# Another order for the copies of finished half tiles and for the first gate and up products in a hybrid decoder layer

## The chip, the cores and the metric

The kernel runs on one core of one Trainium2 chip. The metric is the device time of one execution in microseconds. Below, TensorE is PE (its weight loads PEld), VectorE is DVE, ScalarE is ACT, GpSimd is POOL, and SP issues the DMAs. A time difference of about 0.2% is what a measurement of this kernel can tell from none.

## What is computed

One decoder layer on 1024 tokens of width 1024, in float32. The mixing part has three groups of heads; the rest is a gated feed-forward part:

```python
h = rms_norm(x, ln_attn_pre[l])
mix = hybrid_mixer(h, w_in[l], ...)   # NSA | sliding window | stick-breaking heads
x = x + rms_norm(mix @ w_out[l], ln_attn_post[l])
h = rms_norm(x, ln_ffn_pre[l])
f = (jax.nn.silu(h @ ffn_w_gate[l]) * (h @ ffn_w_up[l])) @ ffn_w_down[l]
x = x + rms_norm(f, ln_ffn_post[l])
```

Stick-breaking heads need a log, a scan along the keys and an exponential per row; the window and selection heads need a softmax.

## The kernel before

Every float32 product is made of three products of rounded parts: high by high, high by low, low by high. So each operand is cut: ACT writes the high part, DVE subtracts it from the source and writes the low part. TensorE then runs six or twelve matmuls of 512 columns on them.

**Projection.** `h @ w_in` is computed transposed, in 13 column tiles of 128 output features and two halves of 512 tokens each: 26 halves. A half is four pieces of six matmuls (`piece`, L916), all into one PSUM bank, and from the eleventh half on every half uses the same bank 6. Each half that is finished is copied out of PSUM by ACT (`half_keep`, L1133), scaled by POOL (`half_scale`, L818), and, for keys, cut again. So the first piece of the next half waits until that copy is made (`pe.wait_ge(half_kept, ...)`). The weights of a tile are loaded in two items, whose high parts ACT cuts (`cut_hi`, L1117) and whose low parts DVE makes (`cut_lo`, L1304); three items are held, so a `cut_hi` waits until the pieces of the item three before are done. An item ends at the end of a half or two pieces before it, so in every second case the same piece releases a `half_keep` and a `cut_hi`.

**Attention.** The later halves are interleaved with the attention jobs: `scores` (L997 to L1005), for stick-breaking `stick_exp` (ACT, L1214), `stick_log` (ACT, L1221), `stick_soft` (DVE, L1415), `stick_scan` (DVE, L1423), `stick_sub` (DVE, L1430), `stick_weights` (ACT, L1226); for the others `logits` (DVE, L1407) and `softmax` (ACT, L1202). Then `turn` (PE transposes, L1032), `keep` (a copy to SBUF by ACT, L1232, or DVE, L1437), `weigh` (PE, L1052) and `combine` (DVE, L1467 or L1473). Near the end come the cuts of `w_out`: `out_hi` (ACT, L1266), `out_lo` (DVE, L1497), the first four of which are released by the last piece.

The order of all this on each engine is not written out but planned when the program is built. `plan_attention` lists every item with its engine, an assumed cost, what it needs, and a number called its age. It then always takes the item that can begin first, and among those that can begin at the same time the one with the lowest age:

```python
begin = max(at, free_at[e] if e != "dma" else at)
key = (begin, work[k][3], k)
```

The cuts of the projection's weights and the copies of its halves all have age -100, attention items have ages that grow with the job. With equal ages the name decides, and `cut_hi` comes ahead of `half_keep`. Some of the `keep` items may go to ACT or DVE, whichever is free first by the plan. Each engine then runs its list in that order and waits by semaphores; the numbers of the plan play no part any more.

**Feed-forward.** Gate and up products are done with a seven-product scheme on 2x2 blocks (`P1` to `P7` for each of 22 units, `product`, L2409), down products in the same manner (L2439). The products P1 and P2 of the first four units come first, since they need only tokens that are ready early. The last token tile's transposes (`turn(NT - 1)`, L2343) stand between the fourth product and the fifth. Here the order on ACT and DVE is written by hand, ahead of the loop over all products:

- ACT: `cut_hi` (L1956, high part of weights for one product), `top_cut` (L1933, high part of sums of token blocks), `hidden_raw` (L1905, copies the turned last token tile out of PSUM), `block_hi` (L1914), `snap_first` (L1964, copies P1 of a unit out of PSUM), `silu_first` (L1977), and in the loop `snap_second` (L1969, copies the P6 bank out).
- DVE: `cut_lo` (L2194), `top_rest` (L2188, low parts of the sums), `sums` (L2129 to L2137, the sums themselves), `hidden_cut` (L2119), `first_block` (L2201, adds P2 to P1). The second product P2 in a bank waits for the `first_block` two units before it.

The sixth product needs `first_block(0)`, the eighth `first_block(1)`, the ninth (P6 of unit 0) six of the ten `top_rest`, the tenth (P7) eight, the eleventh (P5) `snap_second(0)`.

## Time and profile before

| | us |
|---|---|
| runs (three) | 1263.75, 1264.02, 1265.2 |
| median | 1264.02 |
| the profiled execution | 1261.04 |
| its span, first to last instruction | 1259.2 |
| mean granted TensorE clock in it | 0.997 |
| busy in it: PE, DVE, ACT, POOL | 1231.5, 866.3, 602.8, 179.1 |

The span is what the rows count; 1.84 us of the profiled execution lie outside it, and that execution was 2.98 us shorter than the median. Times in rows are from the start of the span. In a row of a timeline the first number is the start, the second the duration; the bracket at the end gives the engine's idle time before it and who ended it. "x" is a count.

By the timeline, the first part of the projection runs from 9 us to about 106 us, attention with the interleaved halves from 121 to 520 us, the output product from 520 to 606 us, the gate and up products from 606 to about 1030 us, the down products to 1250 us.

### The profile page before, as it was taken

To read this page: it belongs to the slowest core of one execution; us is meant where nothing else is said; L and a number is where in the kernel's file an instruction comes from. 1 tells how busy PE (TensorE), PEld (TensorE's weight loads), DVE (VectorE), ACT (ScalarE), POOL (GpSimd) and SP (SyncE) were. 2 spreads that over 40 slices of the span, in tenths; PEclk is the share of its full clock that TensorE was granted. 3 is DMA by queue.
4 is the path that set the end of the run, shared out by engine and by line. 5 is a ranking of instruction groups with operands and counts; after the bars stand their busy time and mean duration, and the time that the engine had idled before them with its cause. 6 is when DMAs were issued, how large, how long until landed. Compare 5 with 4: busy or idle time off the path is not lost.

```text
span 1259.2 us, 19142 instructions
## 1 busy us (share of the span) xinstructions
PE 1231.5 (98%) x6744; PEld 1055.9 (84%) x6744; DVE 866.3 (69%) x1656; ACT 602.8 (48%) x1144; POOL 179.1 (14%) x153
## 2 busy tenths in 40 slices
PE   8999999999999999999999999999999999999998
PEld 7899878889988999888778888888888887888886
DVE  6323688859779666355976766656756668796995
ACT  5432677657666565344643333333333436443341
POOL 5230111111100000011001112111212120000104
PEclk9999999999999999999999999999999999999999
DMA  6303512136743000223213333233232367373343
GB/s 233 119 1 119 117 35 51 34 109 169 171 115 88 18 18 18 79 89 115 103 42 109 97 112 100 75 119 125 93 117 85 129 213 275 102 241 93 109 159 134
DMA packets 67171, 136.44 MB, mean 108 GB/s; under 512 B 8663, under 2 KB 27359, under 8 KB 67076
## 3 DMA queue, kind: packets, MB, share of 16 engines
q1 hardware_dynamic: 67076, 135.22, 34.3%
q8 instruction: 54, 0.88, 0.3%
q14 instruction: 41, 0.34, 0.1%
HBM read 89.81 MB, written 28.60 MB: 94 GB/s over the span
## 4 chain that ended last, share of the span: by engine, by line
PE 84%; DVE 8%; issue 3%; ACT 3%; DMA 1%; SPq 0%; POOL 0%; DVEq 0%; POOLq 0%; ACTq 0%
PE ps L2409 32%; PE ps L2439 15%; PE ps L1052 7%; PE ps L2353 6%; PE ps L1032 4%; PE ps L897 4%; PE ps L916 4%; PE ps L842 3%; PE ps L997 2%; PE ps L1005 2%; DVE ring L1423 2%; PE ps L931 1%; PE ps L1063 1%; DVE ring L1415 1%; DVE m_rows_sb L1430 1%
## 5 line engine op out<-in xcount | busy, mean ns | idle before, releaser
L2409 PE MATMUL ps<-f_topH,f_W 128*128 128x512 f32 x704 | 220.8, 389 | 0.8 <-ACT QT L1969 0.8
L2409 PEld LDWEIGHTS ps<-f_topH,f_W 128*128 128x128 f32 x704 | 132.1, 188 | 28.6 <-DVE f_W L2194 1.1
L2409 PE MATMUL ps<-f_topL,f_W 128*128 128x512 f32 x352 | 136.9, 389 | 0.0
L1052 PE MATMUL ps<-V,m_tw 128*128 128x66 f32 (+1 forms) x1056 | 129.6, 271 | 2.7 <-DVE m_mix_n L1467 1.7
L1052 PEld LDWEIGHTS ps<-V,m_tw 128*128 128x128 f32 x1056 | 126.5, 192 | 4.5 <-DVE m_mix_n L1467 2.5
L2439 PE MATMUL ps<-f_headH,f_W 128*128 128x512 f32 x408 | 128.0, 390 | 0.0
L2409 PE MATMUL ps<-f_headH,f_W 128*128 128x512 f32 x352 | 115.0, 390 | 2.4 <-DVE f_p1a L2201 2.4
L2194 DVE TENSOR_TENSOR f_W<-f_scr,f_W 128x512 fp32r<-128x512 f32 x88 | 62.1, 708 | 78.6 <-ACT f_W L1956 78.4
L2194 DVE TENSOR_TENSOR f_W<-ring,f_W 128x512 fp32r<-128x512 f32 (+1 forms) x84 | 76.0, 914 | 46.2 <-ACT f_W L1956 46.2
L2439 PEld LDWEIGHTS ps<-f_headH,f_W 128*128 128x128 f32 x408 | 76.6, 188 | 15.9 <-DVE f_headL L2237 0.2
L2409 PEld LDWEIGHTS ps<-f_headH,f_W 128*128 128x128 f32 x352 | 66.1, 188 | 16.4 <-issue 2.8
L2439 PE MATMUL ps<-f_headL,f_W 128*128 128x512 f32 x204 | 79.4, 389 | 0.0
L2409 PEld LDWEIGHTS ps<-f_topL,f_W 128*128 128x128 f32 x352 | 66.1, 188 | 13.6
L1232 ACT COPY m_tw<-ps 128x512 f32<-128x512 f32 (+1 forms) x97 | 53.5, 567 | 49.6 <-PE ps L1052 28.2
L2409 PE MATMUL ps<-f_headL,f_W 128*128 128x512 f32 x176 | 68.5, 389 | 0.0
L2439 PE MATMUL ps<-f_b22H,f_W 128*128 128x512 f32 x208 | 66.6, 392 | 0.9 <-DVE QT L2229 0.9
L916 PE MATMUL ps<-m_hH,m_wH 128*128 128x512 f32 x144 | 60.3, 419 | 4.9 <-ACT QT L1133 4.8
L2229 DVE TENSOR_TENSOR QT<-ps,QT 128x512 f32<-128x512 f32 x67 | 46.0, 687 | 27.4 <-PE ps L2439 27.3
L2353 PE MATMUL ps<-o_w,o_mH 128*128 128x512 f32 x224 | 60.5, 392 | 0.0
L2409 PE MATMUL ps<-f_b22H,f_W 128*128 128x512 f32 x176 | 57.8, 389 | 0.0
L916 PE MATMUL ps<-m_hH,m_wL 128*128 128x512 f32 x144 | 57.2, 397 | 0.0
L916 PE MATMUL ps<-m_hL,m_wH 128*128 128x512 f32 x144 | 56.9, 395 | 0.0
(288 smaller groups left out, 2727.9 us busy)
## 6 DMA issues: line engine op xcount, KB each, us to landing
act_pairs<-QT SPq DMA_DIRECT2D x77, 256.0 KB, 3.9
f_stage<-act_pairs SPq DMA_DIRECT2D x77, 256.0 KB, 2.6
m_qs<-m_qn SPq DMA_DIRECT2D x128, 128.0 KB, 2.4
ring<-in_ffn_w_up SPq DMA_DIRECT2D x22, 512.0 KB, 3.7
ring<-in_ffn_w_gate SPq DMA_DIRECT2D x19, 512.0 KB, 5.0
ring<-in_w_in_tiles SPq DMA_DIRECT2D x9, 512.0 KB, 3.6
ring<-in_nsa_phi_w SPq DMA_DIRECT2D x8, 512.0 KB, 4.7
ring<-in_w_out SPq DMA_DIRECT2D x8, 512.0 KB, 5.0
```

Of the source, the lines that this page charges most:

```text
L842: return pe.matmul(ps[:, h, :], w[:, k % W_ITEMS, (h // 2) * P:(h // 2 + 1) * P], a[:, k, half_cols(h)], start=first, stop=last)
L897: ins = pe.matmul(ps[:, b + a, 0:VW_HALF], h[:, k, tok], wv[:, w, k, a * VW_HALF:(a + 1) * VW_HALF], start=(k == 0 and h is hH and w == 0) ...
L916: ins = pe.matmul(ps[:, bank, :], w[:, n % W_ITEMS, cols], a[:, k, hf * HALF:(hf + 1) * HALF], start=(k == 0 and w is wH and a is hH), sto ...
L997: pe.matmul(out, q_hi_, k, start=True, stop=False)
L1032: ins = pe.transpose(ps[:, bank, i * P:(i + 1) * P], rows, ident[:])
L1052: ins = pe.matmul(ps[:, SUMS, wide * i:wide * (i + 1)], tw[:, t % W_SLOTS, P * i:P * i + P], v, start=(kb == 0 and i == 0), stop=(kb == jo ...
L1232: act.copy(out, src).then_inc(kept_by["act"], 1)
L2194: dve.tensor_tensor(slots[s % W_RING][:, 1, 0:n], source(s), slots[s % W_RING][:, 0, 0:n].bitcast(F32), ALU.subtract).then_inc(lo_done, 1)
L2229: dve.tensor_tensor(part, product_, part, ALU.add).then_inc(y_added, 1)
L2353: ins = pe.matmul(ps[:, 2 * (t % 2) + hf, :], m[:, t % 2, k, :], w[k][:, a, hf * HALF:(hf + 1) * HALF], start=(k == 0 and m is mH and a == ...
L2409: ins = pe.matmul(ps[:, bank, :], whole[:, w, cols], halves[h][:, k0 + k, col:col + HALF], start=(begins and k == 0 and w == 0 and h == 0) ...
L2439: ins = pe.matmul(ps[:, bank, :], whole[:, w, k * P:(k + 1) * P], block(n)[h], start=(begins and k == 0 and w == 0 and h == 0), stop=(k == ...
```

## The change

Two things, no instruction is added or taken away.

1. In the planner, `half_keep` on ACT gets the age -200 in place of -100. A finished half is now copied ahead of a `cut_hi` that could begin at the same time. Since the planner takes one item after the other, all that comes behind moves too: the lists of all five engines are different from about 130 us to 500 us. Two more of the 164 `keep` items go to ACT and two fewer to DVE.
2. In the hand-written order at the start of the feed-forward part, ACT cuts the weights of the sixth and seventh product ahead of the last token tile, and DVE adds the first block ahead of some sums and low parts.

```diff
@@ plan_attention @@
-            add(("half_keep", h), "act", act(HALF), [("piece", s), ...], -100)
+            add(("half_keep", h), "act", act(HALF), [("piece", s), ...], -200)
             add(("half_scale", h), "pool", 1650, [("half_keep", h)], -100)
@@ act_program @@
         top_cut(2)
         cut_hi(4)
+        cut_hi(5)
+        top_cut(3)
+        cut_hi(6)
+        snap_first(1)
         hidden_raw(NT - 1)
         block_hi(NT - 1)
-        cut_hi(5)
-        top_cut(3)
-        snap_first(1)
         top_cut(4)
-        cut_hi(6)
+        cut_hi(7)
         top_cut(5)
-        cut_hi(7)
-        silu_first(0)
         cut_hi(8)
         top_cut(6)
+        silu_first(0)
+        cut_hi(9)
         top_cut(7)
         snap_first(2)
-        cut_hi(9)
@@ dve_program @@
         normalise(t)
+        cut_lo(4)
+        first_block(0)
         sums(2, (1,))
-        cut_lo(4)
+        cut_lo(5)
         top_rest(1)
-        top_rest(2)
+        cut_lo(6)
         sums(3, (0,))
-        cut_lo(5)
         hidden_cut(t)
         sums(3, (1,))
-        first_block(0)
-        cut_lo(6)
+        top_rest(2)
+        first_block(1)
+        cut_lo(7)
         top_rest(3)
+        sums(2, (2,))
         top_rest(4)
-        cut_lo(7)
         top_rest(5)
-        first_block(1)
-        sums(2, (2,))
         cut_lo(8)
         sums(3, (2,))
         top_rest(6)
+        cut_lo(9)
         top_rest(7)
-        cut_lo(9)
```

How it moves the instructions at three places:

**The end of a half in the stick-breaking stage.** On TensorE, at the end of the sixteenth half (half 15) and the start of half 16; - is before, + is the change. L916 are the pieces, L1052 is `weigh`, L997 to L1005 are `scores`:

```order
 L1002 MATMUL ps<-m_mask_sb,m_identr 128x128
 L1005 MATMUL ps<-m_KSb,m_qs 128x512
-L1052 MATMUL ps<-V,m_tw 128x64 x4
+L1052 MATMUL ps<-V,m_tw 128x64 x8
+L916 MATMUL ps<-m_hH,m_wH 128x512
+L916 MATMUL ps<-m_hL,m_wH 128x512
+L916 MATMUL ps<-m_hH,m_wL 128x512
+L916 MATMUL ps<-m_hH,m_wH 128x512
+L916 MATMUL ps<-m_hL,m_wH 128x512
+L916 MATMUL ps<-m_hH,m_wL 128x512
 L916 MATMUL ps<-m_hH,m_wH 128x512
 L916 MATMUL ps<-m_hL,m_wH 128x512
```

The last piece of half 15 stood earlier, among the transposes of an attention job; now it is directly ahead of the first piece of half 16. On ACT the copy of half 15 (L1133) and the weights' high part beside it (L1117), before:

```order
L1221 ACTIVATE ring<-ring 128x768
L1232 COPY m_tw<-ps 128x512
L1117 CAST m_wH<-ring 128x512
L1133 ACTIVATE QT<-ps 128x512
L1232 COPY m_tw<-ps 128x512 x3
L1232 COPY QT<-ps 128x2x128
L1226 ACTIVATE m_rows_sb<-m_rows_sb 128x768 x2
```

and now:

```order
L1242 COPY m_mix_a<-ps 128x256
L1214 ACTIVATE ring<-ps 128x256
L1252 ACTIVATE m_junk,m_ss<-m_mix_a 128x256
L1133 ACTIVATE QT<-ps 128x512
L1117 CAST m_wH<-ring 128x512
L1221 ACTIVATE ring<-ring 128x768
```

The copy now stands ahead of the cut, and both stand behind the squares of a mixed tile (L1252) instead of ahead of three `keep` copies.

**The cuts of w_out.** On ACT, where the smallest jobs of the last family begin; L1266 is `out_hi`, before:

```order
L1252 ACTIVATE m_junk,m_ss<-m_mix_a 128x512
L1202 ACTIVATE m_rows_cmp<-m_rows_cmp,m_neg 128x15 x4
L1266 CAST o_w<-ring 128x1024
L1196 CAST m_qn<-QT 128x2x128
L1266 CAST o_w<-ring 128x1024
L1232 COPY m_tw<-ps 128x512
L1232 COPY m_tw<-ps 128x256
L1266 CAST o_w<-ring 128x1024
L1202 ACTIVATE m_rows_win<-m_rows_win,m_neg 128x256 x4
L1266 CAST o_w<-ring 128x1024
L1202 ACTIVATE m_rows_slc<-m_rows_slc,m_neg 128x256 x4
```

and now:

```order
L1202 ACTIVATE m_rows_slc<-m_rows_slc,m_neg 128x128 x3
L1266 CAST o_w<-ring 128x1024
L1202 ACTIVATE m_rows_slc<-m_rows_slc,m_neg 128x128
L1266 CAST o_w<-ring 128x1024 x2
L1196 CAST m_qn<-QT 128x2x128
L1266 CAST o_w<-ring 128x1024
L1232 COPY m_tw<-ps 128x256
L1252 ACTIVATE m_junk,m_ss<-m_mix_a 128x512
L1202 ACTIVATE m_rows_cmp<-m_rows_cmp,m_neg 128x15 x4
```

The four `out_hi` stood between the `keep` copies and the softmax rows of 128x256; now they stand ahead of the rows of 128x15. The four `out_lo` on DVE moved ahead in the same way.

**The first feed-forward products.** On DVE, behind the normalising of the last token tile; L2194 is `cut_lo`, L2188 `top_rest`, L2201 `first_block`, L2129 to L2137 `sums`:

```order
 L2129 TENSOR_TENSOR QT<-QT 128x4x128
 L2108 SCALAR_TENSOR_TENSOR o_tmp<-ring,o_rs,o_gpre 128x1024
+L2194 TENSOR_TENSOR f_W<-f_gates,f_W 128x512
+L2201 TENSOR_TENSOR f_p1a<-ps,f_p1a 128x512
 L2133 TENSOR_TENSOR QT<-QT 128x4x128
 L2194 TENSOR_TENSOR f_W<-f_gates,f_W 128x512
-L2188 TENSOR_TENSOR f_topL<-QT,f_topH 128x8x128 x2
+L2188 TENSOR_TENSOR f_topL<-QT,f_topH 128x8x128
+L2194 TENSOR_TENSOR f_W<-f_gates,f_W 128x512
 L2129 TENSOR_TENSOR QT<-QT 128x4x128
-L2194 TENSOR_TENSOR f_W<-f_gates,f_W 128x512
 L2119 TENSOR_TENSOR f_b22L<-QT,f_b22H 128x4x128
```

`first_block(0)` moved ahead of three sums, two low parts of 128x8x128, a `cut_lo` and a `hidden_cut`, and the low parts follow later, one by one.

## Rows read from the trace of the kernel before

**Rows 1.** The page: busy time, share of the span, instructions.
```profile
PE 1231.5 (98%) x6744; PEld 1055.9 (84%) x6744; DVE 866.3 (69%) x1656; ACT 602.8 (48%) x1144; POOL 179.1 (14%) x153
```

**Rows 2.** View of waits, TensorE: who for whom, total us, times, longest.
```profile
PE ps L916 <- ACT QT L1133: 4.8, 4, 2.3
PE ps L2409 <- DVE f_p1a L2201: 2.4, 1, 2.4
...
PE ps L1052 <- DVE m_mix_n L1467: 1.7, 2, 1.1
...
PE ps L1052 <- ACT m_tw L1232: 0.9, 1, 0.9
...
PE ps L1032 <- ACT m_rows_win L1202: 0.7, 1, 0.7
```

**Rows 3.** Stretches: busy us of each engine (x instructions), PEclk, DMA share, GB/s.
```profile
121.00:270.00 149.00, 141.14 (x828) 120.41 (x828) 119.86 (x157) 101.01 (x208) 24.82 (x20) 0.99 0.25 63
270.00:360.00 90.00, 89.76 (x693) 84.55 (x692) 69.09 (x263) 58.20 (x152) 8.45 (x12) 1.00 0.63 153
360.00:370.00 10.00, 9.65 (x71) 8.69 (x71) 6.70 (x31) 5.71 (x17) 0.54 (x1) 1.00 0.25 58
370.00:395.00 25.00, 20.88 (x155) 18.67 (x154) 24.35 (x99) 19.52 (x46) 1.08 (x2) 1.00 0.54 158
...
606.00:640.00 34.00, 30.89 (x140) 25.06 (x139) 31.89 (x47) 24.47 (x39) 1.84 (x2) 1.00 0.22 78
```

**Rows 4.** Timeline of TensorE: first products behind an idle time, 170 to 262 us.
```profile
175.49 0.48 PE L916 MATMUL ps<-m_hH,m_wH 128*128 128x512 f32 x1 [1.35 <-ACT QT L1133]
...
190.96 0.47 PE L916 MATMUL ps<-m_hH,m_wH 128*128 128x512 f32 x1 [1.00 <-ACT QT L1133]
...
232.55 0.47 PE L916 MATMUL ps<-m_hH,m_wH 128*128 128x512 f32 x1 [2.28 <-ACT QT L1133]
...
260.06 0.30 PE L997 MATMUL ps<-m_KSa,m_qs 128*128 128x128 f32 x1 [1.19 <-DVE m_rows_sb L1430]
```

**Rows 5.** Timeline of ACT just ahead of the third of them.
```profile
231.31 0.60 ACT L1117 CAST m_wH<-ring 128x512 fp32r<-128x512 f32 x1
231.81 0.59 ACT L1133 ACTIVATE QT<-ps 128x512 f32<-128x512 f32 x1
```

**Rows 6.** Stretch behind the third, columns as in rows 3.
```profile
233.00:237.00 4.00, 4.00 (x13) 3.08 (x12) 3.97 (x5) 0.95 (x1) 1.07 (x1) 0.57 0.00 0
```

**Rows 7.** Timeline of POOL and of DVE at two half ends.
```profile
232.48 1.59 POOL L818 TENSOR_TENSOR QT<-QT 128x512 f32<-128x512 f32 x1 [2.96 <-ACT QT L1133]
...
232.92 1.70 DVE L1304 TENSOR_TENSOR m_wL<-ring,m_wH 128x512 fp32r<-128x512 f32 x1
...
175.44 0.68 DVE L1304 TENSOR_TENSOR m_wL<-ring,m_wH 128x512 fp32r<-128x512 f32 x1
```

**Rows 8.** Timeline of ACT, 370 to 372 us.
```profile
370.23 1.04 ACT L1266 CAST o_w<-ring 128x1024 fp32r<-128x1024 f32 x1
371.18 0.85 ACT L1232 COPY m_tw<-ps 128x512 f32<-128x512 f32 x2
```

**Rows 9.** Timeline of DVE, 391 to 394 us.
```profile
391.63 1.22 DVE L1497 TENSOR_TENSOR o_w<-ring,o_w 128x1024 fp32r<-128x1024 f32 x1
393.17 0.42 DVE L1467 TENSOR_TENSOR m_mix_n<-ps,m_coef 128x256 f32<-128x256 f32 x1
```

**Rows 10.** Timeline of TensorE in the first feed-forward products: idle times.
```profile
622.95 0.47 PE L2409 MATMUL ps<-f_headH,f_W 128*128 128x512 f32 x1 [2.36 <-DVE f_p1a L2201]
...
637.55 0.47 PE L2409 MATMUL ps<-f_topH,f_W 128*128 128x512 f32 x1 [0.75 <-ACT QT L1969]
```

**Rows 11.** Timeline of DVE and ACT around them.
```profile
622.12 0.69 DVE L2201 TENSOR_TENSOR f_p1a<-ps,f_p1a 128x512 f32<-128x512 f32 x1
...
634.55 0.68 DVE L2201 TENSOR_TENSOR f_p1b<-ps,f_p1b 128x512 f32<-128x512 f32 x1
...
636.83 0.57 ACT L1969 COPY QT<-ps 128x512 f32<-128x512 f32 x1
```

More of the change, by code:

```diff
@@ L244, in plan_attention @@
         elif s % 4 == 3:
-            add(("half_keep", h), "act", act(HALF), [("piece", s), ("half_lo", h - 10 if kind == "k" else 21) if h >= 20 else None], -100)
+            add(("half_keep", h), "act", act(HALF), [("piece", s), ("half_lo", h - 10 if kind == "k" else 21) if h >= 20 else None], -200)
             add(("half_scale", h), "pool", 1650, [("half_keep", h)], -100)
```

## The prediction

> **What bounds it now.** I read the page's totals first, then the waits of TensorE, the busy times by stretch, and the timeline at each wait. TensorE is busy 98% of the span [rows 1], and the change adds and removes no instruction, so the time can change only by TensorE's idle time, by its clock, and by little else. The stretches say where idle time is left: 7.9 us between 121 and 270 us (149.00 less 141.14), 0.2 in the next 90 us, 0.4 from 360 to 370, 4.1 from 370 to 395, and 3.1 from 606 to 640 [rows 3]. These are the places that the two edits touch. Elsewhere a new order moves work that TensorE hides.
>
> **Ends of halves, 121 to 270 us.** TensorE waited 4.8 us in four places for the copy of a half [rows 2]: 1.35 us at the opening of half 14, 1.00 at half 15, 2.28 at half 18 [rows 4], which leaves 0.2 for the fourth, at half 12. At the third ACT made the weights' cut at 231.31 and began the copy at 231.81 [rows 5]: the cut ahead of it costs 0.5 us. Behind that wait the clock was 0.57 of full over 4.00 us [rows 6], that is, it stood at 1.2 in place of 2.4 GHz for most of it, which costs 4.00 x 0.43 = 1.7 us of work. Now, half by half, from the order of the changed kernel:
> - Half 12: the cut is behind the copy, the wait of 0.2 goes: -0.2.
> - Half 14: the cut is behind, -0.5, and one `scores` pair of about 0.5 us now stands in the gap: -1.0 of 1.35.
> - Half 15: no cut stood ahead of the copy, 0.
> - Half 18: the copy loses the cut, -0.5, so 1.8 us stay. The clock did not fall behind 1.35 us here (0.99 over the stretch is the one fall) [rows 3, 4], nor behind 2.36 us at 622.95, where it is 1.00 [rows 3, 10], but did behind 2.28. I take it as gone: -1.7. Its other end is 0.
> - Halves 16 and 22: work stood between the last piece of the half before and the first of these; now there is none. Each costs a bare opening, 1.00 us as at half 15 [rows 4]: +2.0.
> - Half 20 is now directly behind half 19 too, but there TensorE stood 1.19 us for the scores anyway [rows 4]: -0.2. Half 21 opens behind only 0.6 us of scores: +0.4. Together +0.2.
>
> Sum -0.2 - 1.0 - 0.5 - 1.7 + 2.0 + 0.2 = **-1.2 us**. From 270 to 360 us TensorE has no idle time [rows 3], so what is won before arrives at 360 unabridged.
>
> **The cuts of w_out, 360 to 395 us.** DVE is full there, 24.35 of 25.00 us, and had 3.3 us free in the ten before [rows 3]. By the new order the last piece stands ahead of the last eight `scores` before it and releases the four `out_hi` (1.04 us each, [rows 8]) and `out_lo` (1.22, [rows 9]) earlier. Behind them stood: the copy of a transposed block at 371.18, directly behind an `out_hi` [rows 8], waited for 0.9 us; softmax rows, 0.7; and two combines, one at 393.17 behind an `out_lo` at 391.63 [rows 9], together 1.7 [rows 2]. So 3.3 us of TensorE's idle time stand directly behind a cut. Against it: the pieces that filled TensorE up to there end sooner, and two `out_lo`, 2.4 us, now stand ahead of the last combine of the sliding-window jobs, for which TensorE must wait; half of that, 1.2 us, I take as new idle time. -3.3 + 1.2 = -2.1, rounded to **-2.0 us**. The ends: all of 4.1 + 0.4 gone, -4.5; or all of the 2.4 new and only one of the cuts' waits gone, +1.5.
>
> **POOL beside DVE.** Each copy releases POOL's scaling. At 232.48 POOL began 0.44 us ahead of DVE's low part, and that took 1.70 us; at 175.44 DVE began together with it and took 0.68 [rows 7]. With the copy ahead of the cut, POOL begins first each time: 1.0 us more on DVE at five half ends or so (9, 11, 13, 19, 21), 5 us at most. TensorE waits for DVE rarely there (1.19 us at half 19 is the one large wait in rows 4), so I put **+0.5 us** on the path; the ends are 0 and +5. The Trainium skill, page "SBUF — State Buffer", section "Who interferes with whom", says that a VectorE instruction with two SBUF inputs and a GpSimd one that reads SBUF lock each other out, and the one issued first holds the shared ports to its end; by that rule every one of the five is paid in full, and the rows agree for the two places shown. It speaks against this change, and is a rival below.
>
> **First feed-forward products, 606 to 640 us.** TensorE waited 2.36 us ahead of the sixth product for `first_block(0)`, made at 622.12, and 0.75 ahead of the eleventh for `snap_second(0)` [rows 10, 11]. The edit puts the first block ahead of seven other DVE items, and cuts the sixth product's weights inside an idle time of ACT, so the wait of 2.36 goes. But what is late next? The eleventh product waits for ACT's copy at 636.83; ahead of that on ACT stands a silu that needs `first_block(2)`, which DVE began at 634.55 [rows 11]. Between the normalising of the last tile and 634.55 DVE has the same instructions before and after, only in another order, and it is the full engine: 31.89 of 34.00 us [rows 3]. So `first_block(2)` comes at about the same time, and so do the copy and the eleventh product. The idle time moves: Stepping the new DVE list from the normalising on, with 0.6 to 0.7 us for a 128x512 item [rows 11] and 1.2 for a 128x1024 one [rows 9], the eighth low part is there after 16.8 us, and TensorE at the tenth product, with five products of 12 matmuls behind the last tile's turn, after 15.5: I expect 1.3 us idle ahead of the tenth and the other 1.8 ahead of the eleventh. Only a DVE idle moment can be won: **-0.2 us**. The ends are -0.7 (the wait of 0.75 goes) and +1.7 (a clock fall as in rows 6, for two near waits in place of one).
>
> **Sum.** -1.2 - 2.0 + 0.5 - 0.2 = -2.9 us. The profiled execution took 1261.04, so its like would take 1258.1; the median of the runs lies 2.98 above it: 1264.02 - 2.9 = **1261.1 us**. About 0.2%, 2.5 us, is what a measurement can tell from none; the bound is 1261.5, so this is barely a gain.
>
> **Rivals.**
> 1. *The full DVE only passes its idle time on.* The cuts of w_out delay the last sliding-window combines as much as they free the later ones; the term of -2.0 is 0: 1263.1. For it: DVE is full at 370 to 395 and its total does not change [rows 3]. Against: 3.3 free us just ahead. Chance 0.23.
> 2. *POOL's lock on the path.* All five low parts pay 1.0 and stick-breaking rows wait behind them: the term is +5 in place of +0.5, 1265.6. For it: rows 7. Against: TensorE waits little for these rows [rows 4]. Its rule is that of the page named above. Chance 0.10.
> 3. *Slower: bare openings as at half 18.* If ACT is busy with stick-breaking rows when halves 16 and 22 end, each wait is 2.28 and not 1.00, and if the clock falls behind both as in rows 6, each costs 1.7 more: 2 x (1.28 + 1.7) = +6.0, so 1267.1. It decides from a wait of about 2.3 us on, since 1.35 left the clock alone. For it: ACT is busy 101 of 149 us there [rows 3]. Against: half 15 opened bare with 1.00. Chance 0.13.
> 4. *The change doesn't do what it says.* The plan's costs are assumed; if ACT is in fact free whenever a half ends, copy and cut differ by 0.5 us that nobody waits for, and the rest is chance: 1264.0. Against: at half 18 the cut did stand ahead [rows 5]. Chance 0.06.
>
> **Numbers.** The forecast has 0.48; its own range by the terms is 1257 to 1261.5. Faster by more than 0.2%: 0.48. Within: 0.23 + 0.10 + 0.06 = 0.39. Slower: 0.13. The range leaves out the end of rival 3 and the case in which all of 4.5, 2.9 and 0.7 goes: 1256.5 to 1266.0.
>
> **What would show it.** In the new profile: the wait for the copy of a half at half 14 is at most 0.4 us and at half 18 below 1.8, with full clock behind it; new waits of about 1 us stand at halves 16 and 22. Idle time from 121 to 270 us is some 8 us. From 360 to 395 TensorE idles some 2.5 us in place of 4.5, with no `out_hi` behind 368 us. There is no wait ahead of the sixth product, two ahead of the tenth and eleventh with about 3 us together, and the eleventh begins as long after the last tile's normalising as before, within 0.3 us. The low parts beside POOL take 1.7 us. The prediction is wrong if the sum of TensorE's idle time falls by less than 2 us, or more than 6, or if the change is found where I see none, behind 395 us.

## The result, and the profile after

The changed kernel is slower: 1266.37 us at the median of 20 runs, against 1263.74 for 20 runs of the kernel before on the same chips. The ratio is 1.0024 with a 95% interval of [1.0016, 1.0032]. The prediction was 1261.1.

The executions list a mean granted clock each, so time can be split for all of them. I call **clock loss** the span times one minus that clock, and **rest** the time less the clock loss. Half of any idle time that passes while the clock is down counts as loss. The figures are means over the executions of a kernel, without one of about 2070 us of the change and one of x6:

| | executions | mean time | clock loss | rest |
|---|---|---|---|---|
| before (the runs beside the experiments) | 128 | 1263.3 | 6.2 | 1257.1 |
| after | 19 | 1266.6 | 8.5 | 1258.1 |

Of 3.3 us, 2.3 are clock and 1.0 is the rest. The standard error is 0.4 and 0.2 us for the change. The 128 executions were taken on four chips, whose means are 1262.3, 1263.1, 1263.5 and 1263.9 us (rest 1257.0, 1256.7, 1257.2, 1257.3). So a difference of under 1 us between means of different chips shows little, and each ratio below is to before on the same chip.

The profiled execution of the changed kernel took 1269.17 us (span 1267.4, clock 0.991), longer than its median. Its busy times, as in [rows 1]:

```profile
PE 1237.9 (98%) x6744; PEld 1061.6 (84%) x6744; DVE 863.5 (68%) x1654; ACT 604.5 (48%) x1146; POOL 181.3 (14%) x153
```

Its stretches, as in [rows 3]:

```profile
121.00:270.00 149.00, 140.41 (x824) 119.05 (x823) 116.53 (x155) 102.13 (x210) 26.04 (x20) 1.00 0.26 64
270.00:360.00 90.00, 88.40 (x675) 82.32 (x673) 67.99 (x250) 56.48 (x147) 8.51 (x12) 1.00 0.61 152
360.00:370.00 10.00, 8.63 (x72) 8.07 (x71) 8.21 (x32) 7.57 (x16) 0.00 (x0) 1.00 0.49 141
370.00:395.00 25.00, 20.30 (x134) 19.03 (x134) 19.76 (x85) 14.54 (x37) 2.00 (x2) 0.80 0.44 134
...
606.00:640.00 34.00, 34.00 (x159) 28.06 (x157) 31.95 (x44) 22.66 (x35) 2.41 (x4) 1.00 0.27 97
```

From 121 to 270 us the clock is full now, and idle time is 8.6 us, where it was 7.9. From 360 to 395 it is 6.1, where it was 4.5, and the clock has fallen to 0.80. From 606 to 640 there is none, because this part now runs some 8 us later: its waits lie at 641 and 645 us (below). The waits of TensorE, as in [rows 2]:

```profile
PE ps L916 <- ACT QT L1133: 5.5, 8, 1.0
PE ps L1021 <- DVE m_mix_a L1487: 3.5, 1, 3.5
PE ps L997 <- DVE m_rows_sb L1430: 3.1, 4, 1.5
PE ps L1052 <- ACT m_tw L1232: 2.2, 2, 2.1
PE ps L2409 <- ACT QT L1969: 1.6, 1, 1.6
...
PE ps L2409 <- issue: 1.0, 1, 1.0
```

The second line is new. The third was 1.9 us before, the fourth 0.9 [rows 2]. The one wait of 3.5 us is for the norm of the last sliding-window tile (`norm_mix`, L1487), whose transposes (L1021) TensorE runs next. The timeline of TensorE around it:

```profile
370.69 0.69 PE L1052 MATMUL ps<-VC,m_tw 128*128 128x132 f32 x4 [2.06 <-ACT m_tw L1232]
...
376.21 1.09 PE L1021 MATMUL ps<-ident,m_mix_a 128*128 128x128 f32 x4 [3.48 <-DVE m_mix_a L1487]
```

and the stretches there, two microseconds each:

```profile
370.00:372.00 2.00, 1.31 (x10) 1.34 (x11) 1.33 (x11) 1.96 (x8) 0.00 (x0) 0.92 0.96 324
372.00:374.00 2.00, 0.73 (x4) 0.44 (x3) 1.93 (x6) 0.00 (x0) 0.26 (x1) 0.50 0.76 303
374.00:376.00 2.00, 0.00 (x0) 0.00 (x0) 1.48 (x2) 0.00 (x0) 1.20 (x1) 0.50 0.69 242
...
380.00:382.00 2.00, 2.00 (x11) 2.00 (x11) 1.78 (x11) 1.34 (x4) 0.00 (x0) 0.52 0.00 0
```

The clock goes to 0.50, 1.2 in place of 2.4 GHz, at 371.7 us (0.92 from 370 to 372 us). That is 1 us behind the end of the first wait, of 2.06 us, and 1 us ahead of the second, of 3.48. It stays down through the second wait and for nearly 6 us of work behind it: the matmuls from 376.2 to 381.9 us take twice their time, which is 2.9 us. So in this execution the norm's wait did not bring the clock down by itself; it stood in a time in which the clock was down already.

The first wait comes from the high parts on ACT. The copy that TensorE waits for stands directly behind the last of four `out_hi`:

```profile
369.24 1.04 ACT L1266 CAST o_w<-ring 128x1024 fp32r<-128x1024 f32 x1
370.18 0.36 ACT L1232 COPY m_tw<-ps 128x256 f32<-128x256 f32 x1
```

Why is the norm late? The chain is combine (L1467), squares (ACT, L1252), mean (L1479), root (POOL, L822), norm (L1487). DVE before:

```profile
364.76 0.42 DVE L1467 TENSOR_TENSOR m_mix_a<-ps,m_coef 128x256 f32<-128x256 f32 x1
...
367.30 0.75 DVE L1487 SCALAR_TENSOR_TENSOR m_mix_a<-m_mix_a,m_rs,m_g_w 128x512 f32<-128x512 f32 x1 [0.73 <-POOL m_rs L822]
```

DVE after:

```profile
366.87 2.47 DVE L1497 TENSOR_TENSOR o_w<-ring,o_w 128x1024 fp32r<-128x1024 f32 x2 [0.15 <-ACT o_w L1266]
...
369.66 0.42 DVE L1467 TENSOR_TENSOR m_mix_a<-ps,m_coef 128x256 f32<-128x256 f32 x1
...
371.64 1.22 DVE L1497 TENSOR_TENSOR o_w<-ring,o_w 128x1024 fp32r<-128x1024 f32 x1
...
373.52 0.14 DVE L1479 TENSOR_SCALAR m_ms<-m_ss 128x1 f32<-128x1 f32 x1
373.58 1.22 DVE L1497 TENSOR_TENSOR o_w<-ring,o_w 128x1024 fp32r<-128x1024 f32 x1
375.31 0.75 DVE L1487 SCALAR_TENSOR_TENSOR m_mix_a<-m_mix_a,m_rs,m_g_w 128x512 f32<-128x512 f32 x1 [0.52 <-POOL m_rs L822]
```

From the end of the combine to the end of the norm it took 2.87 us before, 5.98 after, and the combine itself came 4.90 us later. Two low parts stand ahead of the combine, one ahead of the mean, one behind it. The last one hits the root. POOL before and after:

```profile
366.65 0.54 POOL L822 TENSOR_TENSOR m_rs<-m_ms,m_mhalf 128x1 f32<-128x1 f32 x1 [10.44 <-DVE m_ms L1479]
```

```profile
373.74 1.46 POOL L822 TENSOR_TENSOR m_rs<-m_ms,m_mhalf 128x1 f32<-128x1 f32 x1 [14.89 <-DVE m_ms L1479]
```

The root works on one number per partition. It took 0.92 us more beside a low part that had begun 0.16 us ahead of it, and ended 0.40 us behind that part's end. This is the rule of the Trainium skill, "SBUF — State Buffer", "Who interferes with whom", in the direction that I had not looked at: DVE was first and POOL waited.

And nothing covered it. Before, the last piece of the projection (103) stood in the list of TensorE directly ahead of these transposes, and piece 102 six items ahead of it. The norm ended at 368.05 and the transposes began at 368.72, as soon as the piece was through: no wait, and 0.7 us of slack. Now the last piece ends at 365.34, and from there TensorE has only what hangs on DVE and ACT.

The openings of halves, as in [rows 4]:

```profile
175.43 0.47 PE L916 MATMUL ps<-m_hH,m_wH 128*128 128x512 f32 x1 [0.68 <-ACT QT L1133]
...
207.43 0.47 PE L916 MATMUL ps<-m_hH,m_wH 128*128 128x512 f32 x1 [1.03 <-ACT QT L1133]
...
215.65 0.50 PE L997 MATMUL ps<-m_KSb,m_qs 128*128 128x512 f32 x1 [1.55 <-DVE m_rows_sb L1430]
...
233.07 0.47 PE L916 MATMUL ps<-m_hH,m_wH 128*128 128x512 f32 x1 [0.78 <-ACT QT L1133]
```

And the feed-forward part, as in [rows 10]:

```profile
641.08 0.47 PE L2409 MATMUL ps<-f_topH,f_W 128*128 128x512 f32 x1 [1.02 <-issue]
...
645.71 0.47 PE L2409 MATMUL ps<-f_topH,f_W 128*128 128x512 f32 x1 [1.62 <-ACT QT L1969]
```

### The profile page after: what moved, and what is told of

Its sections match the earlier page's. It is cut to its first block, busy times and chain, and to the rows that moved or that the text cites. A ratio compares the mean times of both kernels' runs of the same rounds, so it can differ in the third digit from the quotient of the medians.

```text
span 1267.4 us, 19142 instructions
## 1 busy us (share of the span) xinstructions
PE 1237.9 (98%) x6744; PEld 1061.6 (84%) x6744; DVE 863.5 (68%) x1654; ACT 604.5 (48%) x1146; POOL 181.3 (14%) x153
## 4 chain that ended last, share of the span: by engine, by line
PE 82%; DVE 9%; issue 3%; ACT 2%; DMA 2%; POOL 1%; SPq 1%; DVEq 0%; POOLq 0%; ACTq 0%
PE ps L2409 31%; PE ps L2439 15%; PE ps L1052 8%; PE ps L2353 4%; PE ps L916 4%; PE ps L1032 4%; PE ps L897 4%; PE ps L842 3%; PE ps L997 3%; PE ps L1005 2%; PE ps L931 1%; DMA m_qs<-m_qn 1%; DVE ring L1423 1%; PE ps L1063 1%; DVE ring L1415 1%
## 5 line engine op out<-in xcount | busy, mean ns | idle before, releaser
L1052 PE MATMUL ps<-V,m_tw 128*128 128x66 f32 (+1 forms) x1056 | 131.9, 274 | 0.4 <-ACT m_tw L1232 0.2
L1052 PEld LDWEIGHTS ps<-V,m_tw 128*128 128x128 f32 x1056 | 128.9, 194 | 3.0 <-issue 0.7
L2194 DVE TENSOR_TENSOR f_W<-f_scr,f_W 128x512 fp32r<-128x512 f32 x88 | 62.1, 708 | 78.2 <-ACT f_W L1956 78.1
L2194 DVE TENSOR_TENSOR f_W<-ring,f_W 128x512 fp32r<-128x512 f32 (+1 forms) x84 | 76.0, 914 | 46.9 <-ACT f_W L1956 46.9
L916 PE MATMUL ps<-m_hH,m_wH 128*128 128x512 f32 x144 | 60.2, 418 | 5.5 <-ACT QT L1133 5.5
L1956 ACT CAST f_W<-ring 128x512 fp32r<-128x512 f32 (+1 forms) x84 | 50.6, 606 | 13.7 <-PE ps L2439 9.8
L818 POOL TENSOR_TENSOR QT<-QT 128x512 f32<-128x512 f32 x24 | 34.4, 1446 | 156.1 <-ACT QT L1133 147.6
```

Source lines behind the costliest of these rows:

```text
L916: ins = pe.matmul(ps[:, bank, :], w[:, n % W_ITEMS, cols], a[:, k, hf * HALF:(hf + 1) * HALF], start=(k == 0 and w is wH and a is hH), sto ...
L1052: ins = pe.matmul(ps[:, SUMS, wide * i:wide * (i + 1)], tw[:, t % W_SLOTS, P * i:P * i + P], v, start=(kb == 0 and i == 0), stop=(kb == jo ...
L1956: act.copy(slots[s % W_RING][:, 0, 0:n], source(s)).then_inc(hi_done, 1)
L2194: dve.tensor_tensor(slots[s % W_RING][:, 1, 0:n], source(s), slots[s % W_RING][:, 0, 0:n].bitcast(F32), ALU.subtract).then_inc(lo_done, 1)
```

## The experiments

Below, the *tail* is the end of the sliding-window jobs, 360 to 400 us, and a *bare opening* is the first piece of a half directly behind the last piece of the half before, with no other work between. The expectations name theories. **T1**: the early cuts of w_out make the last sliding-window norm late, and the clock falls. **T2**: the bare openings of halves cost the time. **T3**: the last pieces come too early and no longer cover the norm. **F**: the feed-forward edit only moves idle time and wins about 0.4 us. **C**: a late norm costs its wait and, mostly, a clock fall. **I**: idle time only. **O**: the opening of half 16 costs the time. Each kernel ran 12 times, beside the kernel before on the same chip. In x3, x6 and x8 line numbers are one higher than in the change, in x11 two; in x9, x10 and x13 they are two higher from L1487 on.

| | ratio to before [95%] | mean | clock loss | rest | norm wait | waits 360–400 |
|---|---|---|---|---|---|---|
| before | 1 | 1263.3 | 6.2 | 1257.1 | 0 | 4.4 |
| after | 1.0024 [1.0016, 1.0032] | 1266.6 | 8.5 | 1258.1 | 3.48 | 6.0 |
| x1 ffn edit only | 0.9977 [0.9962, 0.9993] | 1260.9 | 4.7 | 1256.2 | 0 | 4.2 |
| x2 plan edit only | 1.0034 [1.0019, 1.0050] | 1267.9 | 10.7 | 1257.3 | 2.59 | 5.2 |
| x3 cuts held | 1.0036 [1.0018, 1.0054] | 1268.5 | 7.4 | 1261.1 | 1.88 | 6.2 |
| x4 halves under 16 | 1.0002 [0.9985, 1.0019] | 1263.8 | 4.2 | 1259.6 | 0 | 4.8 |
| x5 halves from 16 | 1.0021 [1.0009, 1.0034] | 1266.3 | 7.8 | 1258.5 | 3.88 | 6.7 |
| x6 pieces held | 1.0018 [1.0004, 1.0032] | 1265.5 | 5.3 | 1260.2 | 1.35 | 4.4 |
| x7 half 13 only | 0.9996 [0.9985, 1.0007] | 1262.6 | 6.0 | 1256.6 | 0 | 4.2 |
| x8 low parts held | 1.0009 [0.9999, 1.0018] | 1264.3 | 5.8 | 1258.5 | 1.33 | 4.7 |
| x9 norm late, 20 spare | 1.0000 [0.9987, 1.0014] | 1263.2 | 6.5 | 1256.7 | 1.93 | 6.1 |
| x10 norm late, 10 spare | 0.9992 [0.9980, 1.0005] | 1262.3 | 4.9 | 1257.3 | 0.60 | 5.0 |
| x11 both held | 1.0012 [0.9997, 1.0027] | 1264.8 | 4.0 | 1260.8 | 1.34 | 4.7 |
| x12 all but half 15 | 1.0024 [1.0009, 1.0040] | 1265.8 | 8.2 | 1257.6 | 3.54 | 6.1 |
| x13 norm late, 40 spare | 1.0037 [1.0020, 1.0054] | 1267.2 | 7.6 | 1259.6 | 4.49 | 7.8 |
| x14 halves under 15 | 0.9997 [0.9983, 1.0010] | 1261.9 | 3.7 | 1258.2 | 0 | 4.2 |

The last two columns are of the profiled execution: the wait ahead of the transposes L1021 of the last sliding-window tile, and all waits of TensorE over 0.2 us from 360 to 400. Standard errors of x1 to x14: 0.4 to 0.8 us for the clock loss (1.0 in x3), 0.2 to 0.55 for the rest. Means include all executions, and the first row is the mean of four chips, so means can stand some tenths off the ratio.

**x1 and x2: the two edits apart.** x1 has the hand-written lists of the change and the old age (the diff shows it against the change); x2 has the new age and the lists of before.

```diff
-            add(("half_keep", h), "act", act(HALF), [("piece", s), ("half_lo", h - 10 if kind == "k" else 21) if h >= 20 else None], -200)
+            add(("half_keep", h), "act", act(HALF), [("piece", s), ("half_lo", h - 10 if kind == "k" else 21) if h >= 20 else None], -100)
```

> Only the second edit (the order of the first feed-forward products); the planner as before. Theory F (the edit moves TensorE's idle time and wins little): 0.4 us less than the kernel before, ratio 0.9997; the waits are about 1.0 us ahead of the tenth product and 1.6 ahead of the eleventh, in place of 2.4 ahead of the sixth. Rival (two near waits lower the clock): 1 to 2 us more than before.

> Only the first edit (the age of the copies of halves). If the slowdown is the planner's alone: 3 us more than the kernel before, ratio 1.0027, with a wait of 3 to 4 us of TensorE for the norm of the last sliding-window tile (DVE m_mix_a L1487) near 376 us. If the two edits hurt together only: within 1 us of before.

The feed-forward edit is a gain by itself, 0.9977 [0.9962, 0.9993]; the plan edit a loss, 1.0034 [1.0019, 1.0050]. The sign lies in the plan. Multiplied, the two ratios give 1.0011, with an error of about 0.0022, where the change has 1.0024: they add up within the noise and no better. x1 is below the 0.9997 of theory F by more than its interval. In x2 the wait for the norm is 2.59 us, under the 3 to 4 expected. The waits of x1 are those of the change in this part, and its rest is 0.5 us and its clock loss 1.7 us under those of before on the same chip:

```profile
630.46 0.47 PE L2409 MATMUL ps<-f_topH,f_W 128*128 128x512 f32 x1 [1.01 <-issue]
...
635.08 0.47 PE L2409 MATMUL ps<-f_topH,f_W 128*128 128x512 f32 x1 [1.65 <-ACT QT L1969]
```

**x3: cuts of w_out held back.** Behind the copy of the turned last sliding-window tile.

```diff
- add(("out_hi", k), "act", act(D), [("out", k), room], 1e5)
+ held = ("keep", lay.turn_at["swa", NT - 1]) if k < OUT_EARLY else None
+ add(("out_hi", k), "act", act(D), [("out", k), room, held], 1e5)
```

> The changed kernel, but the planner may place the first four high parts of w_out only behind the keep copy of the last sliding-window tile; the lists are those of the changed kernel up to there. Theory T1 (the early cuts of w_out make the last sliding-window norm late, and the idle time lowers the clock): the wait of 3.5 us at 376 us and the one of 2.1 us at 371 are gone, the clock stays at 1.00 there, time 0 to 3 us below the kernel before, ratio 0.998 to 1.000. Theory T2 (the bare openings of halves 16, 20 and 22 cost the time): still 2 to 3 us above before, ratio 1.002.

```profile
370.37 0.63 PE L1022 MATMUL ps<-ident,m_mix_a 128*128 128x128 f32 x4 [1.88 <-DVE m_mix_a L1488]
...
380.83 1.11 PE L1053 MATMUL ps<-V,m_tw 128*128 128x66 f32 x8 [1.36 <-DVE m_mix_n L1468]
...
395.94 0.33 PE L1053 MATMUL ps<-V,m_tw 128*128 128x66 f32 x1 [1.45 <-DVE m_mix_n L1468]
```

No gain: 1.0036 [1.0018, 1.0054]. With no low part in the way the root took 0.54 us, the norm wait fell to 1.88 and the wait of 2.06 us was gone (0.70 for a combine stood there), but the held cuts then stood ahead of later work, and TensorE waited 0.83, 1.36 and 1.45 us for combines. The clock, which T1 wanted at 1.00, fell to 0.50 behind the 1.88 us, from 370.9 to 374.3 us. T1 in its simple form fell. The rest of x3, 3.0 us over that of the change, is not explained by its waits, which are as long.

**x4 and x5: the new age for some halves only.**

The end of the `half_keep` line in x4; in x5 the condition is `h >= 16`:

```diff
-[("piece", s), ("half_lo", h - 10 if kind == "k" else 21) if h >= 20 else None], -200)
+[("piece", s), ("half_lo", h - 10 if kind == "k" else 21) if h >= 20 else None], -200 if h < 16 else -100)
```

> The changed kernel, but the new age only for halves below 16: bare openings at halves 16 and 20, none at 22, and the cuts of w_out stand as in the kernel before. T1: no long wait at 371 to 376 us, time within 1.5 us of before (ratio 0.999 to 1.001). T2: one bare opening fewer of three, so 1.5 to 2 us above before (ratio 1.0012 to 1.0018).

> The changed kernel, with the new age of the copies kept only for halves 16 and later; halves before 16 have the age of before. T3 (new, after the held cuts left 6.2 us of waits in 360 to 400: the last pieces of the last half, which before stood between the turn of the last sliding-window tile and the nsa jobs as filler, are now done before it, and nothing covers the chain combine, squares, mean, root, norm, turn): nearly the whole loss is here, ratio 1.001 to 1.004, a wait of 2.5 to 3.6 us for the norm of the last sliding-window tile near 376, 5.5 to 6.5 us of waits of over 0.2 us in 360 to 400, with a clock fall behind them in most executions. T2 (bare openings at halves 16, 20 and 22): the same order, 1.000 to 1.003, but its waits are near 215, 259 and 283, and those in 360 to 400 explain under 1 us. If the loss needs the halves before 16, the ratio is under 0.999.

x5 has the tail of the change and nearly all of its loss, 1.0021 [1.0009, 1.0034]; its clock loss is 7.8 us, its norm wait 3.88.

x4 has the tail of before and no norm wait, and the lowest clock loss but two, 4.2. Its ratio, 1.0002 [0.9985, 1.0019], is in T1's range and leaves T2's open. Its rest speaks for T2: it is 2.5 us over the one of before, and 3.4 over x1, which ran on the same chip and differs from it by the age of these halves alone. Its timeline shows where:

```profile
206.53 0.47 PE L916 MATMUL ps<-m_hH,m_wH 128*128 128x512 f32 x1 [1.02 <-ACT QT L1133]
...
214.74 0.50 PE L997 MATMUL ps<-m_KSb,m_qs 128*128 128x512 f32 x1 [1.57 <-DVE m_rows_sb L1430]
...
232.75 0.47 PE L916 MATMUL ps<-m_hH,m_wH 128*128 128x512 f32 x1 [1.35 <-ACT QT L1133]
```

The opening of half 16 and the scores behind it wait 2.6 us that were not there before; waits over 0.2 us from 121 to 270 sum to 9.4 us, before 7.2. A further 1.21 us near 302 us is a wait for a DMA of queries, of which more below.

**x6: pieces 102 and 103 held** behind the turns that they followed before.

```diff
+ needs += [("turn", lay.turn_at["swa", NT - 1] - 2 + s - PIECES + 1)] if s >= PIECES - 2 else []
  add(("piece", s), "pe", 6 * 226.5, needs, 1e4 + s)
```

> The changed kernel, with the last two pieces (102 and 103) held in the plan behind the turns that they followed before; the w_out cuts, which need piece 103, then come late too. All other openings are as in the change. T3: the wait for the norm near 376 falls to under 1 us, waits in 360 to 400 sum to 4 to 5 us as before, the ratio is 0.998 to 1.001, that is 2 to 5 us under the change. T2: the early openings cost as they do in the change, ratio 1.001 to 1.004, with the tail repaired for under 1.5 us of it.

The norm wait is 1.35, where T3 wanted under 1, the waits at the tail are those of before in sum (4.4 us), and the clock loss is 3.2 us under the change. But the rest is 2.0 us over it, so that 1.0018 [1.0004, 1.0032] is left, in T2's range and above T3's. Most of the 2.0 may be a matter of counting: in the profiled execution of the change the clock was down for all of the wait of 3.48 us, so 1.7 us of idle time stand there under clock loss, and in x6 none do. T3 has the mechanism of the clock loss, and not the whole time.

**x7: half 13 alone** has the new age.

```diff
-[("piece", s), ("half_lo", h - 10 if kind == "k" else 21) if h >= 20 else None], -200)
+[("piece", s), ("half_lo", h - 10 if kind == "k" else 21) if h >= 20 else None], -200 if h in (13,) else -100)
```

> The changed kernel with the new age for the copy of half 13 alone: pieces in the order of before from half 17 or so on, the w_out cuts as before, the ffn edit in. T3: 0.9965 to 0.999, as the ffn edit alone, tail waits 4 to 5 us. T2: one opening moved to be covered (14), one new bare one (17): within 1 us of the ffn edit alone either way. If the gain of the new age at half 14 that the prediction booked (1.0 us) is real, it is the fastest so far, near 0.997.

0.9996 [0.9985, 1.0007], above all that was expected: the opening of half 14 waits less (0.78 us), but half 17 opens bare for 0.78. The rest is 0.4 us over x1, which is within the noise; of the 1.7 us in the mean 1.3 are clock loss.

**x8: low parts held** behind the norm; **x11: that and the pieces.**

```diff
+ behind = ("norm_mix", 2 * NT - 1) if k < OUT_EARLY else None
- add(("out_lo", k), "dve", dve(D), [("out_hi", k)], 1e5)
+ add(("out_lo", k), "dve", dve(D), [("out_hi", k), behind], 1e5)
```

> The changed kernel with the four low parts of w_out held on VectorE behind the norm of the last sliding-window tile; ScalarE's high parts stay early, and so do the last pieces. T1 in its port form (the root on GpSimd took 1.46 us beside a low part, and VectorE's low parts push the norm back): the root takes about 0.54 us, the wait for the norm falls by 2 to 3 us, ratio 0.999 to 1.002. T3: the root falls to 0.54 us too and the norm wait by about 1.5 us as in the held-cuts kernel, but the idle time goes to later items: 360 to 400 still sums to 5 to 6.5 us and the ratio is 1.001 to 1.004.

```profile
370.67 0.54 POOL L823 TENSOR_TENSOR m_rs<-m_ms,m_mhalf 128x1 f32<-128x1 f32 x1 [12.32 <-DVE m_ms L1480]
```

```profile
372.23 0.63 PE L1022 MATMUL ps<-ident,m_mix_a 128*128 128x128 f32 x4 [1.33 <-DVE m_mix_a L1488]
```

```profile
368.00:370.00 2.00, 0.87 (x8) 0.78 (x7) 1.41 (x10) 2.00 (x4) 0.00 (x0) 1.00 0.92 324
370.00:372.00 2.00, 0.90 (x8) 0.69 (x6) 1.93 (x9) 1.19 (x6) 0.54 (x1) 1.00 0.08 31
```

> The changed kernel with both repairs of the end of the sliding-window jobs: pieces 102 and 103 held behind the turns that they followed before, and the low parts of w_out held behind the norm. The bare openings of halves 15, 16, 20 and 22 stay. Theory C: no norm wait over 1.4 us, clock's loss 5 to 6 us as in the two single repairs (5.3 and 5.8). Time without the clock's loss stays 2 to 3.5 us over the one of before, because of the bare openings; ratio 1.0005 to 1.002. If the openings cost nothing, the ratio is under 0.9995.

x8 undoes the least: the high parts stay early on ACT, the root takes 0.54 us again, the wait is 1.33 in place of 3.48, and the clock stays at 1.00 though TensorE idles 2.2 of 4 us. One thing more moved: the plan gave the copy behind the fourth high part to DVE (L1438), so that the wait of 2.06 us became 1.13. What each of the two shorter waits did for the clock x8 does not tell apart. Clock loss falls by 2.7 us, the mean time by 2.3, the ratio is 1.0009 [0.9999, 1.0018]. The port form of T1 named these numbers; T3, which wanted 5 us of waits from 360 to 400, got 4.7. x11 loses only 4.0 us to the clock (5 to 6 expected), and its rest is 3.7 us over before (2 to 3.5 expected); ratio 1.0012 [0.9997, 1.0027]. So the repairs of the tail give the clock back, and leave time that lies elsewhere; holding the pieces adds to it (x6 and x11 against the change and x8: 2.0 and 2.2 us of rest). The counting above can be 1.7 of the first 2.0; for x11 against x8 it explains nothing, and what those 2.2 us are was not found.

**x9, x10 and x13: a late norm by itself.** The plan of before, the feed-forward edit, and 20, 10 or 40 spare DVE instructions ahead of that one norm.

```diff
+ for q in range(20 if i == 2 * NT - 1 else 0):
+     dve.scalar_tensor_tensor(out=spare[:, 2 * q:2 * q + 2], in0=gain_of(family)[:, 0:2], scalar=rs[:, i:i + 1], in1=gain_of(family)[:, 0:2], op0=ALU.mult, op1=ALU.mult)
```

> The ffn edit alone, with the plan of before, and 20 spare VectorE instructions of 128x2 ahead of the norm of the last sliding-window tile (some 0.15 us each, 3.0 us in all; they write to a buffer that nothing reads). The order of all other work is the one of before. It measures what a late norm at this place costs, by itself. Theory C (a late norm costs its wait and, in most executions, a clock fall): with 0.4 us of slack at the turn, a wait of 2.2 to 2.8 us for the norm near 367, time without the clock's loss up by 2 to 2.8 us on the ffn edit alone, and the clock's loss (span times one minus the mean granted clock) up from 4.7 us to 6.5 or more: ratio 1.0005 to 1.003. Theory I (idle only; where the clock falls has nothing to do with this wait): the clock's loss stays at 4.7 to 5.5 us, ratio 0.9995 to 1.0005. If the wait is made up by later idle time, the ratio stays under 0.999.

> As the kernel with 20 spare instructions, with 10 (1.5 us). A wait of about 1.1 us for the norm. Theory C: time without the clock's loss up by 0.8 to 1.2 us, the clock's loss up by at most 1 us (the waits of 0.9 to 1.4 us at this place in other kernels of this study stood beside a mean loss of 5.3 to 5.8 us). Theory I: the same in idle time, the clock's loss unchanged.

> The ffn edit alone, with the plan of before, and 40 spare VectorE instructions ahead of the norm of the last sliding-window tile (128x1; the 20 of 128x2 gave a wait of 1.93 us at the turn, so some 4.5 us here, or 3 us if the narrower ones are cheaper). Theory C (the late norm brings the clock down): the clock's loss 8 us or more, as in the change (8.5), and a clock fall at 370 to 380 in the profiled run; time in all up by 5 to 7 us on the ffn edit alone, ratio 1.002 to 1.004. Theory I (idle time only): clock's loss 4.5 to 6 us, up by 2.5 to 4.5 us in all, ratio 1.000 to 1.0015.

```profile
370.21 0.63 PE L1021 MATMUL ps<-ident,m_mix_a 128*128 128x128 f32 x4 [1.93 <-DVE m_mix_a L1489]
```

```profile
373.41 0.99 PE L1021 MATMUL ps<-ident,m_mix_a 128*128 128x128 f32 x4 [4.49 <-DVE m_mix_a L1489]
```

```profile
370.00:372.00 2.00, 0.00 (x0) 0.00 (x0) 2.00 (x17) 0.05 (x1) 0.00 (x0) 1.00 0.94 254
...
374.00:376.00 2.00, 1.74 (x8) 1.34 (x7) 2.00 (x4) 1.31 (x3) 0.00 (x0) 0.50 0.04 8
```

Against x1, waits of 0.60, 1.93 and 4.49 us cost 1.4, 2.3 and 6.3 us in the mean, and the clock loss rose by 0.2, 1.8 and 2.9 us. These are means of different chips; by the ratios, each to before on its own chip, the three cost 1.9, 2.9 and 7.6 us. The clock fell behind the wait of 4.49 and not behind 1.93 in the profiled executions. So a norm that is late by itself, with the attention lists as before, makes the kernel as slow as the plan edit did, 1.0037 [1.0020, 1.0054], and nearly half of that is clock. Theory C holds in x13, with a clock loss 0.4 us under the 8 that it wanted. In x9 it had the clock loss (6.5) and not the time: the rest rose by 0.5 us and not by 2, and 1.0000 [0.9987, 1.0014] lies in theory I's range. x10's 1.2 us of rest are twice its wait; its profiled execution also shows two waits for a DMA of queries (1.24 us the longest, near 302 us), as x4 and x6 have and the one of before has not. x9 and x13, whose order is the same up to there, have none, so such waits come and go with the execution, and up to 2 us of a profiled execution's rest can be theirs.

**x12: all but half 15; x14: halves under 15 only.** x12 first:

```diff
-[("piece", s), ("half_lo", h - 10 if kind == "k" else 21) if h >= 20 else None], -200)
+[("piece", s), ("half_lo", h - 10 if kind == "k" else 21) if h >= 20 else None], -100 if h in (15,) else -200)
```

```diff
-[("piece", s), ("half_lo", h - 10 if kind == "k" else 21) if h >= 20 else None], -200)
+[("piece", s), ("half_lo", h - 10 if kind == "k" else 21) if h >= 20 else None], -200 if h < 15 else -100)
```

> The changed kernel with the age of before for the copy of half 15 alone, which opens half 16 later. Theory O (the bare opening of half 16 and the row of scores that then waits, 1.0 and 1.55 us near 207 and 215, are lost time): those two waits shrink by 1.5 to 2.5 us in sum and the time by as much, ratio 1.0005 to 1.002 with the late norm still there (wait of about 3.5 us near 376, clock's loss 8 to 9 us). If they are covered later, as the openings of halves 20 and 22 seem to be, the ratio stays at 1.002 to 1.003.

> The changed kernel with the new age only for halves 14 and earlier. Theory O: with half 15's copy at the age of before, the waits of 1.0 us at half 16's opening (near 207) and 1.55 us at the scores after it (near 215) shrink by 1.5 us or more in sum; the time without the clock's loss falls from 1259.6 (new age for all halves below 16) to 1257.5 to 1258.3, ratio 0.998 to 1.0. If those waits only move to the opening's next place, as they did in the kernel with half 15 alone at its old age (1.53, 0.35 and 0.47 us between 210 and 218), the time without the clock's loss stays above 1258.8 and the ratio at 0.9995 to 1.001.

```profile
205.50 0.47 PE L916 MATMUL ps<-m_hH,m_wH 128*128 128x512 f32 x1 [1.54 <-ACT QT L1133]
...
213.19 0.50 PE L997 MATMUL ps<-m_KSb,m_qs 128*128 128x512 f32 x1 [0.46 <-DVE m_rows_sb L1430]
```

The waits at half 16 did not go, they split: 1.54, 0.34 and 0.46 in place of 1.02 and 1.57. x14's rest is 1258.2, 1.4 under x4 (0.35 standard error), and x12's 0.5 under the change, which is within the noise; the ratio of x12, 1.0024 [1.0009, 1.0040], is that of the change, and that of x14 is 0.9997 [0.9983, 1.0010]. x4 and x14 ran on different chips; measured from before on its own chip, the rest is 2.9 and 1.2 us up, 1.7 apart. So half 15's copy is part of the cost of the early halves in x14, and x12 neither shows nor excludes it in the change; theory O had the rest of x14 right and the waits that should show it wrong. Which opening costs the change its 1 us of rest stays open.

## Why the prediction was wrong

The step that failed is **"the cuts of w_out"**, booked at -2.0 us with +1.5 as its worse end. It named both forces: pieces that end sooner, and two low parts ahead of the last combine. It priced the second as "half of that, 1.2 us" of idle time and stopped at the combine. Behind the combine come squares, mean, root, norm and transposes, on three engines, and low parts stood ahead of the mean and beside the root too. The norm moved from 367.30 to 375.31. Of the 3.3 us that were booked as gone, 2.4 did go: the softmax rows (0.74) and the combines (0.64 and 1.06). The copy behind an `out_hi` did not: the high parts moved ahead of another copy, and its wait rose from 0.92 to 2.06. The norm's 3.48 came on top. So the new idle time was 4.6 us and not 1.2, and in place of -2.0 the waits from 360 to 395 rose by 1.6 us. And this term had no price for the clock behind such waits. In the mean the clock loss is 2.3 us over before; against kernels that, like the change, have no long wait at half 18 but the tail of before (x4 4.2, x14 3.7) it is over 4. In x8, with the low parts held, it is 2.7 us lower.

**Rival 3** had the right sign, near the right time (1267.1) and the right kind of price, a long wait and then a slow clock. Its place was wrong: halves 16 and 22 opened after 1.03 and 0.77 us, as the forecast itself had them. And its rule, that it decides from a wait of about 2.3 us on, does not hold: the clock stayed up behind 2.36 us at 622.95 [rows 10], and it fell behind 1.88 us in x3 and 1.34 and 1.38 us in x6.

**Ends of halves.** Half 14: 1.35 to 0.68, forecast -1.0, was -0.7, so over the 0.4 that the text allowed it. Half 18: 2.28 to 0.78, more than the 0.5 forecast, with the clock at full behind it. Halves 16, 22 and 21: 1.03, 0.77, 0.37 (forecast 1.0, 1.0, 0.4). Half 20: 1.19 to 0.78. Half 15: 1.00 to 0.78, forecast no change. So the openings came out as read or better, except half 14's and a new wait of 0.28 at half 13. What was missing were the scores: 0.82, 0.41 and 1.55 us for stick-breaking rows (L1430), behind openings that had been moved. Waits over 0.2 us from 121 to 270 rose by 1.1 us. From 270 to 360 there were 1.2 us of waits, but 0.77 of them are the opening of half 22, which was booked; 0.45 is a wait for a DMA of queries. So this term failed too, by the scores' waits that nobody booked: x4 has only the early halves of it, and its rest is 3.4 us over x1, where the terms for halves 12 to 16 sum to -0.2.

**The clock behind half 18.** The term of -1.7 held: six profiled executions with a wait of 2.23 to 2.30 us there (before, x1, x7, x9, x10, x13) all show the clock down behind it, and none of those with 1.77 us or less do. The low clock losses of x4 and x14, without such a wait and with the tail of before, agree. But it was lost again at 372 to 382, 5.1 us of clock in the profiled execution, of which 1.7 are half of the idle time.

**POOL beside DVE.** Six of 15 low parts took 1.36 to 1.72 us, their sum rose from 13.3 to 14.9 us. +0.5 was fair, and rival 2 did not come. The wait of one engine for the other came at the root instead, 0.92 us.

**Feed-forward.** As told: no wait ahead of the sixth product, 1.02 and 1.62 us ahead of the tenth and eleventh (forecast 1.3 and 1.8). The eleventh began 19.26 us behind the last tile's turn, 19.70 before: -0.4. By x1 against before on the same chip the gain in the runs is more, 2.2 us, of which 1.7 is clock loss. The change against x2, which differ by this edit alone, has 2.2 us less clock loss too. Where the clock was saved no profile shows, since the profiled executions of before and of x2 had none lost there, so that this part of the gain stays unexplained.

**Numbers.** The measured 1266.37 lies 0.4 above the range. The text's own sign of error, idle time that falls by less than 2 us, came: waits over 0.2 us from 121 to 530 us rose from 12.7 to 16.3. The chance of slower, 0.13, was for one mechanism only. Low parts ahead of a chain with 0.7 us of slack were a second, and the trace of before showed it: the norm's end at 368.05, the transposes' start at 368.72.

## What to carry to other kernels

When an edit releases bulk work earlier, follow the first latency chain that it can stand in front of to its last link, on every engine, and look at what filler used to cover it: here the same edit took the filler away and put the bulk in. A long wait of the matrix engine can cost more than itself: 6.3 us in the mean (7.6 by the ratios) for 4.5 here, with the clock's part in it. And time the parts of a change apart: the half that gains (x1, 0.9977 [0.9962, 0.9993], the fastest kernel here) was hidden behind the half that loses.

## What was not expected of the hardware

The clock falls without a wait too. In the profiled execution of the change, TensorE was busy and the clock went down at 474 us and stayed down for nearly 7 us, as the stretches show:

```profile
472.00:474.00 2.00, 1.78 (x16) 1.67 (x15) 1.58 (x6) 1.25 (x2) 0.00 (x0) 1.00 0.00 0
474.00:476.00 2.00, 2.00 (x12) 2.00 (x12) 0.00 (x0) 0.83 (x1) 0.00 (x0) 0.52 0.03 8
...
478.00:480.00 2.00, 2.00 (x11) 2.00 (x10) 1.39 (x9) 0.94 (x5) 0.47 (x1) 0.50 0.00 0
```

The longest wait in the 20 us ahead of it was 0.22 us. Other executions have such a fall near 54, 100, 450 or 1226 us, or not. Ahead of the one near 1226 stands a wait of 0.5 us. The kernel before, x1, x9, x10 and x13 have one order up to 360 us; in their profiled executions such falls stand at 100 us in before and x9, at 55 in x10, at 53 and 100 in x13, and in x1 there is none. The spread of a kernel's runs is mostly clock: over the 128 executions of before (1258.5 to 1270.0 us) the standard deviation is 2.1 us for the time and 1.9 for the clock loss. The Trainium skill, "TensorE: Matmul & The Clock Gate", section "What's actually happening", says that the gate's watch over the array does not start anew with a kernel, so that at its start the same kernel runs a different number of matmuls at the slow clock from run to run. It speaks of the start; these executions show the same kind of difference later on. Behind a wait of 2.36 us ahead of the sixth product [rows 10] the clock stayed up, behind one of 1.93 in x9 too, and in x3 it fell behind one of 1.88 and in x6 behind one of 1.38 us near 384: the length of one wait alone does not settle it.

A tiny instruction can be held by a large one on another engine: the root on one number per partition took 1.46 us beside a low part of w_out in the change, x2 and x5 (1.45 in x12), and 0.54 or 0.55 in x3, x6, x8 and x11, where none ran beside it.
